# Issuing the recurrence's large-product bank steps in pairs, half as often

## The reference, cut to what matters

```
def step(S, inp):
    r_t, w_t, k_t, v_t, a_t, b_t = inp
    sa = jnp.einsum('bhij,bhj->bhi', S, a_t)
    S = S * w_t[:, :, None, :] + sa[..., None] * b_t[:, :, None, :] + v_t[..., None] * k_t[:, :, None, :]
    return S, jnp.einsum('bhij,bhj->bhi', S, r_t)
...
proj = h @ w_in
```

## Time and profile before

| | |
|---|---|
| median of 3 runs | 3165.95 us (3160.54 to 3171.39) |
| the profiled execution's own time | 3169.78 us |
| its span | 3168.0 us |
| busy share of the span | PE 89%, DVE 46%, ACT 28%, POOL 4% |
| mean granted TensorE clock | 0.946 |

### The profile page before, as it was taken

One profiled execution on the slowest core, in us unless ns is written; L12 is line 12 of the kernel. 1 busy time (PEld: TensorE's weight loads), 2 busy tenths in 40 slices (PEclk: granted clock), 3 DMA queues, 4 the chain that ended last, 5 costly groups with the idle time before them and its releaser, 6 DMA issues.

```text
span 3168.0 us, 48322 instructions
## 1 busy us (share of the span) xinstructions
PE 2805.0 (89%) x21116; PEld 2053.2 (65%) x21116; DVE 1449.4 (46%) x2739; ACT 880.8 (28%) x1432; POOL 118.0 (4%) x197
## 2 busy tenths in 40 slices
PE   6799999998868777783898899999988988999999
PEld 5577777775653332331776677888876666778887
DVE  5554646556551010014466655433356665553433
ACT  3322131313410000002233453322223335432231
POOL 0010101010000000001000000000000000000000
PEclk9899999999978899996999999999999999999999
DMA  4243535353258999994324322333332332323332
GB/s 133 67 152 121 158 102 162 101 155 143 93 234 331 428 428 427 429 428 165 96 82 98 100 89 78 97 100 97 96 85 77 96 77 90 110 80 100 94 99 80
DMA packets 152265, 489.53 MB, mean 155 GB/s; under 512 B 13168, under 2 KB 40432, under 8 KB 139632
## 3 DMA queue, kind: packets, MB, share of 16 engines
q1 hardware_dynamic: 113824, 365.52, 32.3%
q0 software_dynamic: 25840, 94.12, 9.2%
q10 hardware_dynamic: 12384, 26.74, 2.6%
HBM read 456.44 MB, written 29.90 MB: 154 GB/s over the span
## 4 chain that ended last, share of the span: by engine, by line
PE 69%; DVE 12%; DMA 12%; ACT 5%; issue 1%; SPq 0%; POOL 0%; DVEq 0%; ACTq 0%; POOLq 0%
PE psum L156 66%; DMA wslot<-in_w_up 4%; DMA wslot<-in_w_gate 3%; DMA wslot<-in_w_down 3%; PE psum L159 3%; DVE halfL L165 2%; DVE sc__234 L195 1%; ACT halfH L162 1%; DVE m L192 1%; DVE a20S L180 1%; DVE a21S L180 1%; ACT a1S L162 1%; ACT L162 0%; DVE n_xn L168 0%; DVE n_ht L168 0%
## 5 line engine op out<-in xcount | busy, mean ns | idle before, releaser
L165 DVE TENSOR_TENSOR halfL<-ring,halfH 128x1024 fp32r<-128x1024 f32 x302 | 367.5, 1221 | 718.1 <-ACT halfH L162 717.6
L162 ACT ACTIVATE halfH<-ring 128x1024 fp32r<-128x1024 f32 x302 | 316.6, 1053 | 742.6 <-PE psum L156 740.7
L156 PE MATMUL psum<-hH,halfH 128*128 128x512 f32 x1200 | 487.0, 406 | 9.7 <-DVE halfL L165 9.6
L156 PE MATMUL psum<-hL,halfH 128*128 128x512 f32 x1200 | 474.4, 395 | 0.0
L156 PE MATMUL psum<-hH,halfL 128*128 128x512 f32 x1200 | 474.2, 395 | 0.0
L156 PE MATMUL psum<-wslot,XT 128*64 128x512 f32 x1024 | 259.2, 665 | 76.7 <-DMA wslot<-in_w_gate 42.3
L156 PEld LDWEIGHTS psum<-hH,halfH 128*128 128x128 f32 x1200 | 229.2, 191 | 84.9 <-issue 24.0
L156 PEld LDWEIGHTS psum<-hH,halfL 128*128 128x128 f32 x1200 | 229.1, 191 | 49.7
L156 PEld LDWEIGHTS psum<-hL,halfH 128*128 128x128 f32 x1200 | 229.4, 191 | 44.2
L156 PEld LDWEIGHTS psum<-wslot,XT 128*64 128x64 f32 x1024 | 90.4, 152 | 244.7 <-issue 243.5
L156 PE MATMUL psum<-halfH,hH 128*128 128x512 f32 (+2 forms) x576 | 219.3, 381 | 11.8 <-DVE halfL L165 8.4
(11 more groups left out here) (438 smaller groups left out, 3887.4 us busy)
## 6 DMA issues: line engine op xcount, KB each, us to landing
wslot<-in_w_gate SPq DMA_DIRECT2D x32, 2048.0 KB, 29.8
wslot<-in_w_up SPq DMA_DIRECT2D x32, 2048.0 KB, 29.6
wslot<-in_w_down SPq DMA_DIRECT2D x32, 2048.0 KB, 30.1
ring<-in_w_in SPq DMA_DIRECT2D x120, 512.0 KB, 3.8
ada<-in_w_ada POOLq DMA_DIRECT2D x96, 512.0 KB, 4.2
ring<-in_w_gu SPq DMA_DIRECT2D x88, 512.0 KB, 3.6
ring<-in_w_down SPq DMA_DIRECT2D x44, 512.0 KB, 3.8
gate_rows<-stage ACTq DMA_DIRECT2D x48, 256.0 KB, 2.1
```

The lines of the kernel that those rows point to most:

```text
L156: return self.e.matmul(*a, **k)
L162: return self.e.activation(*a, **k)
L165: return self.e.tensor_tensor(*a, **k)
```

## The change

Each call of `more()` now yields two bank steps instead of one (first all sums that are due), and it is called half as often: behind each fourth early step of the front instead of each second, in 9 of the 26 rows instead of 18 (rows 7, 10, 13, 16, 19, 22, 25, 28 and 30), once instead of twice behind the bonus, and behind part 1 of each loop step instead of behind both parts. From row 27 on, two events are taken in a row instead of one.

```diff
--- before.py
+++ after.py
@@ -617,12 +617,12 @@
         n_ada = itertools.count()
 
         def more():
-            if sums:
-                n, j = sums.pop()
+            for n, j in sums:
                 yield "sum", *WOVEN[n][0:2], j
                 if j == 3:
                     events.extend(head_batch(n))
-            for x in next(woven, []):
+            sums.clear()
+            for x in [*next(woven, []), *next(woven, [])]:
                 yield x
                 if x[0] == "spill" and WOVEN[x[1]][0] in "qk":
                     assert not events
@@ -642,14 +642,14 @@
             yield x
             if n == 8:
                 yield "kk", 0, "inverse"
-            if n % 2:
+            if n % 4 == 3:
                 yield from more()
         for pr in range(4):
             yield "begin", pr
             for i in range(5, N_PREP):
                 for d in range(2):
                     yield "prep", pr, d, i
-                if (i - 4) * 18 // 26 > (i - 5) * 18 // 26:
+                if (i - 4) * 9 // 26 > (i - 5) * 9 // 26:
                     yield from more()
                 if pr < 3 and i in (5, 6, 7, 8):
                     yield "kk", pr + 1, ("squares", "sums", "root", "inverse")[i - 5]
@@ -658,15 +658,15 @@
                 if pr and i in (25, 27):
                     yield ("gated", "turned")[(i - 25) // 2], pr - 1
                 yield from ada()
-                yield from event(i > 8)
+                for _ in range(2 if i > 26 else 1):
+                    yield from event(i > 8)
             yield "bonus", pr
             yield from ada()
             if pr == 3:
                 for x in woven:
                     yield from x
             else:
-                for _ in range(2):
-                    yield from more()
+                yield from more()
             early = early_steps(pr + 1) if pr < 3 else iter([])
             for s in range(8):
                 for part in range(2):
@@ -675,8 +675,8 @@
                         x = next(early, None)
                         if x:
                             yield x
-                    if pr < 3:
-                        yield from more()
+                if pr < 3:
+                    yield from more()
                 yield from event(False)
             for x in early:
                 yield x
```

## The result

The changed kernel takes 3198.8 us at the median, against 3165.7 for the kernel before on the same chip: ratio 1.0106, 95% interval 1.0089 to 1.0122. The profiled execution went from 3169.8 to 3197.1 us, by 27.3. I had forecast 3182 (range 3168 to 3198), +16.7 on the profiled execution. The direction was right, the size too small: the median lies 0.8 us above the range. The profiled execution, at 3197.1 us, lies just inside it. Among the four executions of the changed kernel the longest (3205.4 us) has the lowest mean granted clock, 0.938, and the shortest (3187.9) the highest, 0.945.

The account below looks back on a forecast made before the run. TensorE was taken as the bound, busy 554.7 of 569 us over the recurrence. Savings of 9.8 and 10.1 us against waits and clock summed to +16.7, profiled 3186.5, median forecast 3182 (range 3168 to 3198).

Parts of the forecast that it names:

- The clock: TensorE: six new gaps of about 2.7 us, four costing 1.6 each through half clock: +6 us, bounds 0 and 10.
- third rival: Loops, now stretches of only small products: clock falls everywhere, 10 more episodes of 1.6 us, +33, 3199 us. Chance 0.12.
- second rival: Whole kernel: waits come, but the clock doesn't fall and tiles land in time: +4, 3170 us. Chance 0.27.
- Saved in the rows and loops: TensorE: 35 merges in the rows save 9.8 us; 24 loop steps save 0.42 each, 10.1 us.
- Early steps on DVE: Loop steps 2 to 5 of three passes: part 1 waits 0.38 for the second SA, 12 times: +4.6 us.
- The split behind the scans: Loop steps 1 to 2: DVE's low half ends late, so TensorE waits 2.6 for SA, three times: +7.8 us.
- The lora products: Loop step 0: the third product waits 0.4 for ACT without a bank step ahead, three times: +1.2 us.
- The reciprocal: Ahead of row 10, passes 0 to 2: TensorE's wait for DVE grows from 1.15 to 2.75: +4.8 us.
- Two turns in a row: Rows 27 and 28 of passes 0 and 2, row 30 of pass 1: second turn starts later: +4.9 us.
- The ada tiles: Bare rows between pairs: DMA tiles land late, 0.45 a time in 14 places: +6.3 us.
- The front: Front: a bank step fewer gains nothing, costs 1.4 in pass 3; DVE's order gains 0.4: +1.0 us.
- What costs nothing: Sums and spills behind pairs, and norming, scale, gain and rope in bare rows: no cost, covered or absorbed by slack.

Follow-up runs that it names:

- e2: Against the kernel before: pairs of bank steps in the loops only; front, rows and bonus as before. Ratio 1.0033.
- e5: The changed kernel with seven useless matmuls put into TensorE's gaps, with the place in the loops missed. Ratio to before 1.0090.
- e9: The changed kernel with seven useless matmuls ahead of row 10 and, in loop step 2, ahead of part 1. Ratio to before 1.0071.
- e11: The changed kernel with the reciprocal in four quarters behind rows 8 to 11. Ratio to before 1.0065.
- e14: The changed kernel with the reciprocal in quarters and one more pair ending the front (12 bank steps there). Ratio to before 1.0016.
- e4: The changed kernel with the reciprocal's step moved from behind row 8 to behind row 10. Ratio to before 1.0058.
- e13: The changed kernel with one more pair at the end of the front (12 bank steps there). Ratio to before 1.0042.
- e3: The changed kernel with single bank steps behind both parts in loop steps 0 and 1 only. Ratio to before 1.0074.
- e12: The changed kernel with the reciprocal in quarters and single bank steps in loop steps 0 and 1. Ratio to before 1.0054.
- e6: The kernel before with four needless repeats of the clamp on VectorE, lengthening the gap ahead of row 10 in passes 0 to 2. Ratio 1.0035.
- e10: The kernel before with the reciprocal in quarters, front in pairs and one pair behind row 13 for rows 12 and 13, otherwise single. Ratio 1.0014.
- e15: The same as e10 with one single bank step more at the end of the front (11 as before). Ratio to before 0.9986.
- e1: Against the kernel before: pairs in the rows and behind the bonus only; front and loops as before. Ratio 1.0049.

## Why the prediction was wrong, point by point

*The likeliest sum failed in "The clock".* I let four of six gaps cost 1.6 each, +6, with bounds 0 and 10. It measured +18.1, outside my bounds. The gaps were priced nearly right: five of the six had a low clock behind them, 8.5 us of work, inside the bounds. What failed is that I priced the gaps alone and put the clock at the start of the loop at nothing, although it was low there before too. In step 0, where the lora products now follow one another with no bank step between, the lower level stayed for 10.2 us twice, in passes 0 and 2, and the time lost around the start of the loops grew by 10.2 us:

```profile
271.00:275.00 4.00, 3.95 (x16) 1.71 (x16) 0.31 (x2) 0.69 (x1) 0.00 (x0) 0.50 0.00 0
275.00:279.00 4.00, 4.00 (x9) 2.48 (x8) 0.00 (x0) 1.31 (x3) 0.00 (x0) 0.50 0.17 66
```

Such long stretches in the loop's step 0 also come in e2, e5, e9, e11 and e14, in one pass or two, at changing places: in 8 of 24 passes of the eight profiles whose step 0 is paired, and in none of the 27 passes of the nine whose step 0 has single bank steps. So they go with the pair in step 0. What sets them off isn't isolated: the only waits inside step 0 are of 0.5 us and less, e4 and e13 have no such stretch, and no run made that one change alone (e3 and e12 come nearest: they also change step 1). The cause stays open.

*Luck in the rest.* Without the clock my terms add up to +10.7, and the profiled executions give 27.3 - 18.1 = +9.2. That near match is luck. The saving was 8.1 us smaller than forecast, the waits 3.6 smaller, and the front and what follows the recurrence, where I had +1.0, came out 5.0 shorter; the three errors cancel to 1.5.

*My third rival had the number* (10 more episodes, 3199; the low-clock time grew by 39.2 us, as much as 11 to 12 episodes of 3.4). Its reason, stretches of small products, holds for step 0 at most; for the six gaps e5, e6 and e9 show that idle time does it. The rule that stood there, the Trainium skill's (TensorE: Matmul & The Clock Gate, HAM oscillation) picture of an engine that drops to 1.2 GHz between bursts when it waits, agrees with 3 of 3 gaps in e6 and 5 of 6 after the change, for waits of 2.3 to 3.1 us, though the waits in the page's own case are longer, 3 to 5 us. The gaps of 1.15 us ahead of row 10 in the kernel before, which spoke for the second rival, have no low clock behind them, but e3, e10 and e12 show that two such waits close together can.

*Saved in the rows and loops.* Forecast -19.9, measured -11.8. The prices were nearly right: a pair takes 2.95 (forecast 2.92), step 6 takes 4.55 (forecast 4.49), which makes -17.4 of -19.9. The bank step that left the front adds some 1.4 here; I had booked it under the front. And a wait shown as 0.24 costs 0.44 (below): 15 waits for `SA` hide 0.2 each in the busy time, another 3.0. That is -13.0, an estimate; the last 1.2 is within what counting half of the low-clock time leaves uncertain.

*Early steps on DVE.* Forecast 0.38 each (by the forecast's own instants, 1.50 and 1.17, it should have been 0.33). The profile shows 0.24, but a step with early steps takes 4.99 where step 6 takes 4.55: 0.44 each, right in size.

*The split behind the scans.* Forecast 3 x 2.6, measured 2.39, 2.38 and 2.28. The mechanism was right in each instant, its cause was incomplete: I counted the front's lost bank step as 1.4 us in pass 3, and e13 and e15 show that it also put the splits there.

*The lora products.* Forecast +1.2, measured nothing (2.3 us of waits for ACT `slot` in 6 places, as in the earlier trace rows).

*The reciprocal.* Forecast +4.8, measured 8.0 - 3.4 (the `Mrb` waits before) = +4.6.

*Two turns in a row.* Forecast +4.9, measured 5.1 in five waits.

*The ada tiles.* Forecast +6.3 in 14 places, measured 4.9 in 8. Not forecast: 2.0 us for `arow` behind the bonus. Pairing isn't its cause: e10, with single bank steps there, has the same 2.0, and e15 with one more in the front has none. In the kernel before the bonus itself waited for DVE's low half, and ACT made `arow` in that time; the waits for DVE `slot` fell from 5.0 to 2.6 in return.

*The front.* Forecast +1.0, of which 1.4 is a bank step that comes back in pass 3 (above). The front ends at 156.7 instead of 159.7, but half of these 3.0 us arises ahead of its first lora product (at 124.0 instead of 125.5), where nothing was changed. The rest, from 34.2 to 32.7, goes with one bank step fewer. I had taken that step for free cover of a wait, yet TensorE's last wait there only went from 3.14 to 3.44, so it seems to have been on the path. The clock moves the front by more: e1, e2 and e6 have the same front as the kernel before and need 30.8 to 30.9 us for that part, with 20.5 us at the lower level across it where the kernel before has 27.3.

*"What costs nothing".* The z_ss sums, spills and the norming in bare rows cost 0.3 us of waits: right.

## What to carry to other kernels

A filler between dependent steps does two jobs: it hides the wait, and it keeps TensorE from standing idle for so long that the clock drops. When fillers are merged, count the gaps that this opens (here of 2.3 us and more, or two of about 1 us close together), and price each at its length and, by e6 and the clock record, half as much to as much again. And when an interleaved list is re-dealt, look at the phase: one filler more or less ahead of a periodic pattern moves every later side effect of it (here the splits) against the work beside it; e10 and e15 differ in the place of one bank step of 136 and in 0.28% of the time.

## What the runs showed of the hardware

- Gaps of 2.3 to 3.1 us in TensorE's work (waits for `Mrb` or `SA`) brought 3.4 us at 1.2 GHz in 20 cases of 21 (after, e3, e4, e5, e6, e11), what the fillings leave of them, 0.5 to 0.9 (e5 and e9 at row 10, e9 in step 2), in none.
- Two gaps of 1.1 to 1.2 and 0.9 us, 0.6 us apart, were followed by 1.2 GHz in 8 cases of 9 (e3, e10, e12).
- Stretches of 10.2 us at 1.2 GHz came in loop step 0 in 8 of 24 passes with the pair there and in none of 27 without. Their cause is open.
- Useless matmuls in a gap made the kernel faster: e9 by 0.35% against after.
- Idle time understates a wait between small matmuls. They issue 0.12 us apart but each lasts 0.33; the wait of 0.24 in the loop comes on top of the last one's end and costs 0.44 of the step (4.99 against 4.55).
